# Sums of squares of y by block transposes and row sums on VectorE instead of products with ones on TensorE

## The reference, cut to what matters

```python
y = y.reshape(b, s, SSD_INNER) * jax.nn.silu(z.astype(f32))
yg = y.reshape(b, s, SSD_GROUPS, SSD_INNER // SSD_GROUPS)
yg = yg * lax.rsqrt(jnp.mean(yg * yg, axis=-1, keepdims=True) + EPS)
```

## Time and profile before

| what | value |
|---|---|
| median of 3 runs | 1013.82 us (1013.44 to 1014.04) |
| the profiled execution's own time | 1013.7 us |
| its span from first to last instruction | 1012.0 us |
| PE busy | 1003.7 us, 99% |
| DVE busy | 643.1 us, 64% |
| ACT busy | 495.0 us, 49% |
| POOL busy | 134.2 us, 13% |
| granted TensorE clock | full in all 40 slices |

### The profile page before, as it was taken

One profiled execution on the slowest core, in us unless ns is written; L12 is line 12 of the kernel. 1 busy time (PEld: TensorE's weight loads), 2 busy tenths in 40 slices (PEclk: granted clock), 3 DMA queues, 4 the chain that ended last, 5 costly groups with the idle time before them and its releaser, 6 DMA issues.

```text
span 1012.0 us, 13460 instructions
## 1 busy us (share of the span) xinstructions
PE 1003.7 (99%) x5095; PEld 833.4 (82%) x5095; DVE 643.1 (64%) x860; ACT 495.0 (49%) x870; POOL 134.2 (13%) x207
## 2 busy tenths in 40 slices
PE   9999999999999999999999999999999999999997
PEld 8888788778888887888888888988888888888886
DVE  6798898889889888532322333776666666632114
ACT  6668848775885879233112233643343343321121
POOL 6023023302412331000000030200000000000001
PEclk9999999999999999999999999999999999999999
DMA  6434542444355241433232426122343343232312
GB/s 200 148 120 128 172 118 56 154 126 146 95 168 145 73 163 47 135 97 112 84 124 83 166 92 194 47 84 83 89 119 83 85 122 83 84 124 87 121 42 84
DMA packets 119435, 113.36 MB, mean 112 GB/s; under 512 B 14079, under 2 KB 108891, under 8 KB 119387
## 3 DMA queue, kind: packets, MB, share of 16 engines
q1 hardware_dynamic: 119387, 112.72, 36.2%
HBM read 109.94 MB, written 2.77 MB: 111 GB/s over the span
## 4 chain that ended last, share of the span: by engine, by line
PE 81%; DVE 11%; ACT 4%; issue 1%; POOL 1%; DMA 1%; SPq 1%; DVEq 0%; POOLq 0%; ACTq 0%
PE ps L1537 18%; PE ps L1539 18%; PE ps L1538 18%; PE ps L1545 5%; PE ps L1544 5%; PE ps L1546 5%; DVE conv L1157 3%; DVE wlo L1028 2%; PE ps L1665 2%; PE ps L1739 1%; PE ps L1740 1%; PE ps L1741 1%; ACT whi L579 1%; PE ps L1854 1%; PE ps L1865 1%
## 5 line engine op out<-in xcount | busy, mean ns | idle before, releaser
L1028 DVE TENSOR_TENSOR wlo<-raw,whi 128x2048 fp32r<-128x2048 f32 (+2 forms) x82 | 183.8, 2243 | 194.6 <-ACT whi L579 194.4
L1537 PE MATMUL ps<-uhi,whi 128*128 128x512 f32 x768 | 301.0, 392 | 0.0
L1539 PE MATMUL ps<-uhi,wlo 128*128 128x512 f32 x768 | 299.0, 389 | 0.0
L1538 PE MATMUL ps<-ulo,whi 128*128 128x512 f32 x768 | 298.9, 389 | 0.0
L579 ACT ACTIVATE whi<-raw 128x2048 fp32r<-128x2048 f32 (+2 forms) x82 | 153.8, 1877 | 167.2 <-PE ps L1546 93.0
L1537 PEld LDWEIGHTS ps<-uhi,whi 128*128 128x128 f32 x768 | 144.2, 188 | 30.3 <-issue 1.0
L1539 PEld LDWEIGHTS ps<-uhi,wlo 128*128 128x128 f32 x768 | 144.1, 188 | 30.1
L1538 PEld LDWEIGHTS ps<-ulo,whi 128*128 128x128 f32 x768 | 144.2, 188 | 29.4
L1466 DVE SCALAR_TENSOR_TENSOR yT<-ps,fpar,yT 128x511 f32<-128x511 f32 x88 | 65.7, 749 | 36.6 <-ACT yT L985 35.0
L985 ACT ACTIVATE yT<-ps,fpar 128x512 f32<-128x512 f32 x44 | 34.1, 780 | 97.8 <-DVE fpar L1461 68.0
L1537 PE MATMUL ps<-rhi,whi 128*128 128x512 f32 x192 | 74.9, 390 | 0.2 <-DVE rlo L1344 0.2
(11 more groups left out here) (272 smaller groups left out, 1462.4 us busy)
## 6 DMA issues: line engine op xcount, KB each, us to landing
raw<-in_w_in_dram SPq DMA_DIRECT2D x24, 1024.0 KB
raw<-in_w_up_dram SPq DMA_DIRECT2D x44, 512.0 KB
raw<-in_w_down_dram SPq DMA_DIRECT2D x11, 1024.0 KB
sums_bc<-sum_rows_scratch SPq DMA_DIRECT2D x16, 512.0 KB, 3.9
raw<-in_w_ssd_out_dram SPq DMA_DIRECT2D x8, 1024.0 KB
raw<-in_w_in_dram SPq DMA_DIRECT2D x15, 512.0 KB
grow_bc<-sum_rows_scratch SPq DMA_DIRECT2D x12, 512.0 KB, 5.6
raw<-in_w_attn_out_dram SPq DMA_DIRECT2D x4, 1024.0 KB
```

What stands on the lines that cost most here:

```text
L1028: dve.tensor_tensor(wlo[sl][:, 0:width] if into is None else into, raw[sl][:, 0:width], h.bitcast(F32), ALU.subtract).then_inc(s["lo_done" ...
L1537: pe.matmul(bank(b)[:, span], hi_[:, k, c], ah[:, span], start=first and k == ks[0], stop=False)
L1538: pe.matmul(bank(b)[:, span], hi_[:, k, c], al[:, span], start=False, stop=False)
L1539: ins = pe.matmul(bank(b)[:, span], lo_[:, k, c], ah[:, span], start=False, stop=last and k == ks[-1])
```

## The change

The sum over partitions is made without PE. DVE adds the four squared tiles as before, transposes the sum in blocks of 32 x 32 into `conv[:, 1, :]`, and sums each block's 32 columns into 16 numbers per partition (`y_sums`, in `conv[:, 5, 0:64]`). POOL copies the three upper quarters of 32 partitions beside the first, adds the four, scales, adds epsilon and takes the power -0.5 of a 32 x 16 tile. SP writes these 512 numbers to DRAM with a rearranged pattern, and reads them back repeated as before. `norm_sums`, `mean_y` and the first two DMAs are gone. `lo_next(2)` moves ahead of the last part of the rotary arithmetic. `times_dt(1)` moves ahead of `masked_gains`. In the last group the four gate products of y and the last three `split_o` are interleaved. PE's waits on `mean_ok` become waits on `st_ok`, and ACT waits for `sq_red` before its first tap.

```diff
+        y_sums = conv[:, 5, 0:64]
+        y_root = conv[0:32, 5, 64:80]
...
             def spread_roots(g):
-                sp.wait_ge(s["mean_ok"], g + 1)
-                sp.dma_start(mean_scr[g], conv[0:P:32, 5, 0:P]).then_inc(s["means_out"], 16)
-                sp.wait_ge(s["means_out"], 16 * (g + 1))
-                sp.wait_ge(s["root_ok"], g)
-                sp.dma_start(small[:, 16:20], mean_scr[g].rearrange("t c -> (t c)").rearrange("(p j) -> p j", j=NT)).then_inc(s["means_in"], 16)
                 sp.wait_ge(s["root_ok"], g + 1)
-                sp.dma_start(root_scr[g], small[:, 20:24]).then_inc(s["roots_out"], 16)
+                sp.dma_start(root_scr[g].rearrange("(b r) -> r b", r=32), y_root, allow_slow_non_contiguous=True).then_inc(s["roots_out"], 16)
                 sp.wait_ge(s["roots_out"], 16 * (g + 1))
-                sp.dma_start(conv[:, 4, :], root_scr[g].rearrange("p t -> (p t)").partition_broadcast(P)).then_inc(s["roots_in"], 16)
+                sp.dma_start(conv[:, 4, :], root_scr[g].partition_broadcast(P)).then_inc(s["roots_in"], 16)
...
             def root_y(G):
-                pool.wait_ge(s["means_in"], 16 * (G + 1))
-                pool.wait_ge(s["roots_out"], 16 * G)
-                link(pool.tensor_scalar(small[:, 20:24], small[:, 16:20], 4 * EPS, None, ALU.add))
-                pool.tensor_tensor(small[:, 20:24], small[:, 20:24], small[:, 0:1].to_broadcast([P, NT]), ALU.pow).then_inc(s["root_ok"], 1)
+                pool.wait_ge(s["sq_red"], G + 1)
+                for i in range(1, 4):
+                    link(pool.tensor_copy(y_sums[0:32, 16 * i:16 * i + 16], y_sums[32 * i:32 * i + 32, 0:16]))
+                link(pool.tensor_tensor(y_sums[0:32, 0:32], y_sums[0:32, 0:32], y_sums[0:32, 32:64], ALU.add))
+                link(pool.tensor_tensor(y_root, y_sums[0:32, 0:16], y_sums[0:32, 16:32], ALU.add))
+                link(pool.tensor_scalar(y_root, y_root, 1.0 / XW, 4 * EPS, ALU.mult, ALU.add))
+                pool.tensor_tensor(y_root, y_root, small[0:32, 0:1].to_broadcast([32, 16]), ALU.pow).then_inc(s["root_ok"], 1)
...
             def sum_squares(G):
                 dve.wait_ge(s["squared"], G * 4 + 4)
                 for a, b in ((0, 1), (2, 3), (0, 2)):
-                    ins = dve.tensor_tensor(conv[:, a, :], conv[:, a, :], conv[:, b, :], ALU.add)
...
+                    link(dve.tensor_tensor(conv[:, a, :], conv[:, a, :], conv[:, b, :], ALU.add))
+                link(dve.transpose(conv[:, 1, :], conv[:, 0, :]))
+                dve.wait_ge(s["grown"], (G + 1) * (NT - 1))
+                dve.tensor_reduce(y_sums[:, 0:16], conv[:, 1, :].rearrange("p (b c) -> p b c", c=32), AX_X, ALU.add).then_inc(s["sq_red"], 1)
...
                         ins.then_inc(s["roped"], 1)
+                    lo_next(2)
                     dve.wait_ge(s["swap_ok"], 3 * G)
...
-                    lo_next(2)
...
                     maximum()
+                    if t < 2:
+                        times_dt(t)
                     if t == 0:
-                        times_dt(t)
                         dve.wait_ge(s["cbm_ok"], G + 1)
                     masked_gains()
-                    if t == 1:
-                        times_dt(t)
...
-            gate_y(NG - 1)
-            for at in range(5, KD):
-                split_o(at)
+            gate_y(NG - 1, lambda f: split_o(4 + f) if f else None)
...
-            def norm_sums(G):
-
-                pe.wait_ge(s["sq_ok"], G + 1)
-                pe.wait_ge(s["st_ok"], (G + 1) * (NT - 1))
-                for t in range(NT):
-                    ins = pe.matmul(ps[32 * t:32 * t + 32, 7, 0:P], ones[:, 0:32], conv[:, 0, t * P:(t + 1) * P], start=True, stop=True)
-                ins.then_inc(s["norm_mm"], 1)
```

More of the change, by code:

```diff
@@ L173, in hybrid_block @@
             "rows_ok", "rows_out", "sums_in", "grow_in", "fell", "lexp", "grown", "skip_ok", "cb_mm", "cbm_ok", "s_mm", "smx", "sexp", "p_ok", "z_mm", "ztanh", "zg_ok",
-            "m_ok", "pT_mm", "pT_sb", "p_blocks", "p_moved", "off_mm", "scaled", "y_mm", "y_done", "xdt_ok", "xdtd_ok", "st_mm", "st_ok", "gated", "squared", "sq_ok",
-            "norm_mm", "mean_ok", "means_out", "means_in", "root_ok", "roots_out", "roots_in", "yn_ok", "o_mm", "o_sb",
+            "m_ok", "pT_mm", "pT_sb", "p_blocks", "p_moved", "off_mm", "scaled", "y_mm", "y_done", "xdt_ok", "xdtd_ok", "st_mm", "st_ok", "gated", "squared",
+            "sq_red", "root_ok", "roots_out", "roots_in", "yn_ok", "o_mm", "o_sb",
             "split_hi", "split_lo", "ga_mm", "ga_tanh", "at_mm", "at_ok", "gb_mm", "gb_tanh", "so_mm", "so_ok",
@@ L208, in hybrid_block @@
         cw = par[:, 0, 0:NCP].rearrange("p (k t) -> p k t", k=TAPS + 1)
-        mean_scr = nc.dram_tensor("means_scratch", (NG, NT, P), F32).ap()
-        root_scr = nc.dram_tensor("roots_scratch", (NG, P, NT), F32).ap()
+        root_scr = nc.dram_tensor("roots_scratch", (NG, S), F32).ap()
         tab_scr = nc.dram_tensor("rope_scratch", (P, 2, S), F32).ap()
@@ L630, in head_parameters @@
                     act.activation(skip[rows, :], hp[rows, 2, :].rearrange("p (f a) -> p f a", a=2)[:, :, h], ACT.Copy).then_inc(s["hp_ok"], 1)
-            def mean_y(G):
-                act.wait_ge(s["norm_mm"], G + 1)
-                act.activation(conv[:, 5, 0:P], ps[:, 7, 0:P], ACT.Copy, scale=1.0 / XW).then_inc(s["mean_ok"], 1)
             def square_y(G):
@@ L733, in group @@
                         ins.then_inc(s["swap_ok"], 1)
-                if G:
-                    mean_y(G - 1)
                 hi_next(2)
                 act.wait_ge(s["y_mm"], G * NT)
+                act.wait_ge(s["sq_red"], G)
                 tap(0)
@@ L885, in _ @@
                 split_y(k)
-            mean_y(NG - 1)
             for i in range(1, NG):
@@ L1121, in finish_dt, with gate_y @@
                 dve.tensor_tensor(b3(adt[:, :]), dt_s[:, :, :], hp[:, 1, :].unsqueeze(1).to_broadcast([P, NT, NH]), ALU.mult).then_inc(s["dt_ok"], 1)
-            def gate_y(G):
+            def gate_y(G, between=lambda f: None):
                 dve.wait_ge(s["zg_ok"], G * 4 + 4)
@@ L1128, in gate_y @@
                     dve.tensor_tensor(y, y, zg[:, f, :], ALU.mult).then_inc(s["gated"], 1)
+                    between(f)
             def sum_squares(G):
@@ L1764, in group @@
                         half_features(1, f).then_inc(s["qkv_mm"] if f < 2 else s["blk_done"], 1)
-                if G:
-                    norm_sums(G - 1)
                 def conv_tiles(j):
@@ L1777, in conv_tiles @@
                         elif f == 3:
-                            pe.wait_ge(s["mean_ok"], G)
+                            pe.wait_ge(s["st_ok"], G * (NT - 1))
                         elif f > 3:
@@ L1899, in gate_a @@
                 features(3, 1, 1, o).then_inc(s["blk_done"], 1)
-                if first:
-                    norm_sums(NG - 1)
             gate_a(0, True)
@@ L1908, in _ @@
             pe.wait_ge(s["sexp"], NG * NT * (QH + 1))
-            pe.wait_ge(s["mean_ok"], NG)
+            pe.wait_ge(s["st_ok"], NG * (NT - 1))
             with pe.Fori(0, NG // 2) as i:
```

## The result

The changed kernel takes 1018.23 us in the median of 6 runs (1016.3 to 1019.03), the kernel before 1013.68 us in 6 runs beside it: a ratio of 1.004, with a 95% interval of 1.003 to 1.0051. It is 4.5 us slower. The forecast was 1014.4, with a range up to 1016.8, and the time lies above it. The profiled execution took 1018.2 us with a span of 1016.5, 4.5 us over the span before.

A forecast was written before the change was run, and what follows sets the result against it. PE's work and a DVE-ACT chain, only some 0.4 us per group shorter, bound the kernel. 1.45 us late at group 3's tile 1, less 0.3 and 0.55 behind the loop, gave +0.6: 1014.4 us, range 1010.7 to 1016.8.

The forecast's parts named there:

- Roots through DRAM: Roots' write and read back: write between 1.7 and 5.1 us (the far end), roots there before DVE asks, cost nothing.
- The third rival: Roots' write over 6 us makes DVE wait at normalize, each us beyond counting three times: 1022 for 3 more; chance 0.05.
- the loop: PE's turning at tile 1, groups 0 to 3: 0.2 us sooner, then 0.1, 0.8 and 1.45 late.
- the surplus of 0.88 over the cover: DVE's added 1.45 us less its wait for ACT's swapped tile: 0.51 us left in group 1, 0.88 in groups 2 and 3.
- POOL's root: POOL's seven operations instead of two slow DVE's products beside them: 0.1 us per group.
- the second rival: POOL's operations keep DVE's two-input products waiting, the power above all: 1019 to 1032 us, 1015.9 if in part; chance 0.15.
- The first rival: The chain over DVE and ACT has slack and PE keeps everything: 3.1 us off, 1010.7; chance 0.2.
- `lo_next(2)`: Weight block 3's rest made 2.8 us sooner on DVE, as cover so that PE still gets it in time.
- `times_dt(1)`: At tile 1, ahead of the masks: ends PE's waits of 0.24 and 0.30 us, but brings L1290's end 0.11 us later.
- Interleaving: Behind the loop, gates and split_o alternate: about 0.3 us of the attention tile's lateness come back.
- The sign foretold at L1836: If right, PE waits 0.3 to 0.7 us there in groups 1 to 3, which it doesn't today.
- The one foretold at L1682 of tile 1: If right, PE waits 0.3 to 0.7 us at tile 1's turning in groups 1 to 3, which it doesn't today.

The follow-up runs named there:

- e2_load_first: The changed kernel, but in the last group SP starts one more weight block before the roots' write, which stays slow: 1014.57 us.
- e9_rows_write_only: The changed kernel with the roots written as 32 runs of 64 bytes and read without a stride, so they reach tokens in the wrong order: 1014.44 us.
- e7_slow_write_before: The kernel before with only its roots' write changed to 512 runs of 4 bytes (in another, wrong order): 1031.6 us.
- e1_rows_write: The changed kernel with the roots written as 32 runs of 64 bytes and normalize reading the repeated copy with a stride: 1017.77 us.
- e4_no_transpose: e1_rows_write without DVE's block transpose, so the sums are of other rows: 1015.11 us.
- e6_sums_nearly_free: e2_load_first with the block transpose left out and the reduction cut from 512 to 32 columns, so the sums are wrong: 1011.56 us.
- e8_lo_back: e2_load_first with lo_next(2) back at its old place behind the rotary arithmetic for k: 1014.4 us.
- e10_dt_back: e2_load_first with times_dt(1) back behind the masks: 1015.64 us.

## Why the prediction was wrong

**Failed: "Roots through DRAM".** The step that failed is the term "I cost it at nothing". Two things in it were wrong. The write was bounded at 1.7 to 5.1 us and took 6.5 to 7.4. The upper end was a read of 256 KB, and bytes are not what this transfer is made of: in rows of 64 bytes the same 2 KB take 1.3 us. The Trainium skill (DMA: Bandwidth & Descriptors, section "Rules for kernel authors") has one descriptor per element for a last dimension that is not contiguous; the traces agree: with the write in rows the profile counts 118443 packets, with the scattered write 120363, and the difference of 1920 is four times 512 - 32. The prediction drew only "the far end" from it. The other is "SP's next weight load, queued behind the write, has more than 8 us until ACT wants it". In the loop no engine of the changed kernel waits for a weight block's transfer, and I read it there alone. In the last group the write took 7.40 us and PE waited 2.1, so the room there was 7.40 - 2.1 = 5.3 us. The far end of the bound, 5.1, would just have fitted, with 0.2 us to spare; what the write took beyond 5.3 PE paid, and 1.6 us of lower clock came on top. The trace of before had the warning: there ACT stands 3.45 us for this block, so it had no room at all "until ACT wants it", and PE's 2.40 us leave room for a write of 1.41 + 2.40 = 3.8 us, 4.4 with PE's forecast lateness of 0.6. By these rows the far end was not free. (The rest up to 5.3 came from a write that began 0.2 us sooner and a block that took 7.3 us to land and not 8.0.) `e2_load_first` and `e9_rows_write_only` change one thing each, the queue's order or the write's length, and both remove the 3.9 us.

**The third rival** was "roots too late", beginning at 6 us. The write did take over 6, and the roots came in time all the same: they are ready at 130.83, near the early end of the 130.1 to 134.4 foretold, there by about 142.9 (130.9 + 6.7 + 5.3, the last two being medians), and used at 144.96. Some 2 us more would have been needed. Its mechanism is real, as `e7_slow_write_before` shows, where the roots are ready at 134.7; it was not what happened. "Nothing in the trace comes near for 2 KB" was no evidence, since no row had that form.

**Right in its size: the loop.** Forecast at tile 1 of groups 0 to 3: 0.2 sooner, then 0.1, 0.8 and 1.45 late. Measured: 0.28 sooner, 0.10 sooner, 0.41 and 1.35 late. From the first add to the first rotary product DVE takes 124.89 - 121.37 = 3.52 us, where three adds alone stand for 2.14 - 0.09 = 2.05: 1.47, and 1.45 was said. The span from `times_dt` to the end of the `divide` at tile 1 is 182.11 - 178.36 = 3.75, as worked out. The period from group 1 to 2 is 90.59 (90.6 to 90.8 foretold). In the experiments DVE's list was made longer by 1.0 us (`e1_rows_write`) and shorter by 0.7 from there (`e4_no_transpose`), and the periods followed by 1.0 and 0.7. With nearly the whole 1.4 us gone (`e6_sums_nearly_free`) the period of groups 1 to 2 falls by 90.59 - 89.74 = 0.85: the surplus of 0.88 over the cover that was worked out.

The closeness of 1.35 to 1.45 is in part luck. The steps were forecast at 0.7 us each and were 0.51 and 0.94. The 0.4 us more in group 3 enter at one place, DVE's transpose of the probabilities in the last tile of group 2:

```profile
292.72 0.71 DVE L1302 STREAM_TRANSPOSE xdtd<-probs 128x512 f32<-128x512 f32 x1 [0.47 <-DVE probs L1283]
```

L1283 ended at 292.24; in group 1 the same transpose starts 0.11 us behind it. From there on DVE is 0.39 us later than one period of 90.59 us after the same point of group 1. The pause is in `e1_rows_write`, `e2_load_first`, `e8_lo_back`, `e9_rows_write_only` and `e10_dt_back` too, whose last period is longer by 0.3 to 0.4, and it is not in `e4_no_transpose` and `e6_sums_nearly_free`, whose periods are equal. What DVE waits for there is not shown.

**POOL's root.** The 0.1 us per group was 0: the four rotary products beside POOL's additions take 1.72 us and the ones beside its copies 0.68 and 0.69, the length of an undisturbed one. So the second rival is not seen for these small operations. The Trainium skill (SBUF — State Buffer, section "Who interferes with whom") has a DVE instruction with two SBUF inputs contend with a GpSimd one that reads SBUF. The traces agree for large operations only: the two masks at 178.97 take 2.14 us beside POOL's product of 128 x 512, where the earlier trace rows had 1.28. The power took 3.08 us, inside 1.46 to 5.84.

**The first rival**, that PE keeps all, gave 1010.7. `e6_sums_nearly_free` shows its limit with 1011.56.

**`lo_next(2)`** was called necessary cover. The wait of 0.5 to 0.8 us comes without it and costs nothing (`e8_lo_back`): in a loop that another chain bounds, it is only waited earlier. **`times_dt(1)`** did what was said: the waits of 0.24 and 0.30 us are gone, and L1283 comes 0.11 us later (3.75 for 3.64). Put back in the new kernel it costs 0.25 us per group (`e10_dt_back`). **Interleaving** gave 0.14 us of the 0.3.

**Where PE waits.** The sign foretold at L1836 came (L1815 here, 0.57 us more distance and 0.36 of idle time, in three groups). The one foretold at L1682 of tile 1 did not: there PE has no wait, because it has already lost the time at the weighed values of tile 0 (0.31 us), which the prediction does not name, and in group 3 also at L1795 (0.44 more distance, 0.28 idle). All of these are the same lateness of DVE and ACT, met sooner, so the sum at tile 1 stays. But the slack of the chain was read at the wrong place. At tile 1 it was 0.42 us; at the weighed values of tile 0 `pT` ended in group 2 of the kernel before at 264.29 and PE took it at 264.51, and since 0.05 is the least gap in these traces, only some 0.17 us were left there.

The price of the lower clock, 1.6 us, is read from start distances; no experiment separates it from the wait, and only the one execution at a mean granted clock of 1.000 speaks for its size.

## What to carry to other kernels

When a transfer on a queue becomes longer, find what stands behind it in the queue in every stage where it is issued, the last pass of a loop first: there the neighbours are others, and a reading from the steady state does not hold. Ask there how long the engine that takes the block could still have waited for it. Where two loops run side by side within 0.4 us of each other, work taken from one bought nothing here when it was put on the other; move it only where the engine that is relieved sets the pace alone (the last group here). And an experiment that is to take out one cost should be read for the cost that it brings: time it in the trace before its median is believed.

## What the runs showed of the hardware

- A write of 2 KB from SBUF to DRAM took 6.5 to 7.4 us in the changed kernel as 512 runs of 4 bytes from 32 partitions (6.0 to 7.4 over all kernels that have it), 8.0 to 9.5 us from 128 partitions with four each, a median of 1.7 us as 128 runs of 16 bytes, and 1.3 us as 32 runs of 64 bytes. The read back of the same numbers to 128 partitions took a median of 5.3 us after the scattered write, 5.1 after the 128 runs, and 3.3 and 3.2 after the one in rows; why is open.
- After 1.94 us without a matmul PE ran on at full clock for 1.3 us and then at the lower one for about 3.4 us (granted clock 0.51). After 5.37 us without one (`e7_slow_write_before`) it started at the lower one and kept it for 4.6 us.
- One operand of DVE read with a step of 64 bytes made four products of 512 columns 1.04 us longer in the loop, beside POOL's copies (2.85 to 3.89), and 1.5 us longer in the last group (2.49 to 3.99).
- POOL's power of a 32 x 16 tile takes 3.1 to 3.3 us, of a 128 x 4 tile 1.46 us: four times the columns on a quarter of the partitions took twice as long.
